# One more seven-product pair in each of row blocks three and four of a fused decoder layer, with two of their weight sums made ahead on GpSimd and VectorE

## The reference

```python
h = rms_norm(x, attn_norm_g)
proj = h @ w_in                      # 2048 x 10320 columns
q_sb, k_sb, v_sb, q_ds, k_ds, v_ds, q_ix, k_ix, w_ix, g_sb, g_ds = split(proj)
o_sb = stick_breaking_attention(q_sb, k_sb, v_sb)
o_ds = indexed_sparse_attention(rope(norm(q_ds)), rope(norm(k_ds)), v_ds, rope(q_ix), rope(k_ix), w_ix)
merged = sigmoid(g_sb) * (o_sb @ w_branch[:1024]) + sigmoid(g_ds) * (o_ds @ w_branch[1024:])
x = x + merged @ w_out
h = rms_norm(x, ffn_norm_g)
u = causal_depthwise_conv(h @ w_up, conv_w, conv_b)
x = x + (silu(gate(u)) * val(u)) @ w_down
```

## Time and profile before

| | |
|---|---|
| median of the runs | 1425.9 us |
| the profiled execution's own time | 1426.08 us |
| its span, first to last instruction | 1424.4 us |
| PE busy | 1418.9 us (100%) |
| DVE busy | 1203.8 us (85%) |
| ACT busy | 902.8 us (63%) |
| POOL busy | 329.6 us (23%) |
| DMA, mean rate | 262 GB/s |

### The profile page before, as it was taken

How to read it: one execution, slowest core, us unless ns; L and a number is a source line. 1 busy time by engine, 2 the same in 40 slices (tenths; PEclk the granted TensorE clock), 3 DMA queues, 4 the chain that set the end, 5 groups by cost and what they waited for, 6 DMA issues and landing times.

```text
span 1424.4 us, 23622 instructions
## 1 busy us (share of the span) xinstructions
PE 1418.9 (100%) x7583; PEld 1216.2 (85%) x7583; DVE 1203.8 (85%) x1591; ACT 902.8 (63%) x1302; POOL 329.6 (23%) x365
## 2 busy tenths in 40 slices
PE   9999999999999999999999999999999999999998
PEld 7888888888888888888888888888888888888887
DVE  6878998888878767887978888988889879898998
ACT  6546667566767766667665555555555556675775
POOL 2310000423232223560012222323223232100000
PEclk9999999999999999999999999999999999999999
DMA  8776665668999876569778888888888877698896
GB/s 256 243 249 183 208 197 185 194 183 293 312 337 329 285 232 209 186 239 336 258 237 279 275 292 289 279 281 279 290 289 276 280 221 233 232 318 315 312 339 250
DMA packets 151308, 373.22 MB, mean 262 GB/s; under 512 B 14048, under 2 KB 14336, under 8 KB 146768
## 3 DMA queue, kind: packets, MB, share of 16 engines
q1 hardware_dynamic: 150176, 369.93, 77.7%
q0 software_dynamic: 896, 2.42, 0.5%
q10 hardware_dynamic: 176, 0.14, 0.0%
HBM read 333.64 MB, written 38.80 MB: 261 GB/s over the span
## 4 chain that ended last, share of the span: by engine, by line
PE 99%; ACT 0%; DVE 0%; POOL 0%; issue 0%; DVEq 0%; POOLq 0%
PE bank L2320 98%; PE bank L2374 0%; PE bank L2393 0%; PE bank L2598 0%; ACT hT L837 0%; PE bank L2639 0%; DVE y L2008 0%; PE bank L2462 0%; POOL lo L2121 0%; ACT hi L820 0%; PE bank L2440 0%; DVE y L2053 0%; DVEq L243 0%; POOL ident L2101 0%; PE bank L2447 0%
## 5 line engine op out<-in xcount | busy, mean ns | idle before, releaser
L1311 DVE TENSOR_TENSOR lo<-raw,hi 128x1024 fp32r<-128x1024 f32 x338 | 436.6, 1297 | 140.4 <-ACT hi L820 138.6
L820 ACT ACTIVATE hi<-raw 128x1024 fp32r<-128x1024 f32 (+1 forms) x342 | 358.9, 1052 | 262.0 <-PE bank L2320 256.0
L2320 PE MATMUL bank<-h2T,hi 128*128 128x512 f32 x1408 | 483.3, 394 | 0.0
L2320 PE MATMUL bank<-h2T,lo 128*128 128x256 f32 x1408 | 376.8, 278 | 0.0
L2320 PEld LDWEIGHTS bank<-h2T,hi 128*128 128x128 f32 x1408 | 257.9, 188 | 53.5
L2320 PE MATMUL bank<-hT,hi 128*128 128x512 f32 (+1 forms) x784 | 272.9, 395 | 0.1
L2320 PEld LDWEIGHTS bank<-h2T,lo 128*128 128x128 f32 x1408 | 264.5, 188 | 7.8
L2320 PE MATMUL bank<-hT,lo 128*128 128x256 f32 (+1 forms) x784 | 212.6, 281 | 0.0
L1258 ACT ACTIVATE hi<-raw 128x1024 fp32r<-128x1024 f32 (+1 forms) x139 | 132.6, 974 | 64.2 <-PE bank L2320 63.2
L2320 PEld LDWEIGHTS bank<-hT,hi 128*128 128x128 f32 (+1 forms) x784 | 143.9, 187 | 29.8 <-POOL lo L2121 0.5
L1982 DVE TENSOR_TENSOR lo<-raw,hi 128x1024 fp32r<-128x1024 f32 (+1 forms) x139 | 152.2, 1124 | 16.1 <-ACT hi L1258 11.6
(11 more groups left out here) (293 smaller groups left out, 2021.8 us busy)
## 6 DMA issues: line engine op xcount, KB each, us to landing
raw<-in_w_up SPq DMA_DIRECT2D x176, 512.0 KB, 4.6
raw<-in_w_in SPq DMA_DIRECT2D x160, 512.0 KB, 4.6
raw<-in_w_down SPq DMA_DIRECT2D x61, 512.0 KB, 5.7
raw<-sums SPq DMA_DIRECT2D x54, 512.0 KB, 5.8
sums<-pre SPq DMA_DIRECT2D x19, 1024.0 KB, 6.3
raw<-in_w_branch SPq DMA_DIRECT2D x32, 512.0 KB, 4.2
pre<-in_w_down SPq DMA_DIRECT2D x19, 512.0 KB, 5.2
pre<-in_w_down SPq DMA_DIRECT2D x38, 256.0 KB, 5.6
```

The source lines that it names most:

```text
L820: act.activation(hi[s][:, 0:width], raw[s][:, 0:width], ACT.Copy)\
L1311: dve.tensor_tensor(lo[s][:, 0:width], raw[s][:, 0:width], hi[s][:, 0:width].bitcast(f32), ALU.subtract)\
L2320: return pe.matmul(o, l, r, start=start, stop=stop, skip_group_check=True)
```

## The change

Blocks 3 and 4 get five merged pairs instead of four. Two of the five, pairs 2 and 4, are of the stored kind; their weight sums (`ROW_SUMS`, one for each block and pair) are made in blocks 0 and 1 and lie in `row_sums` in DRAM. Two of these four sums are made by POOL (`pool_terms`), ahead of its work on the index keys and behind its first set of index queries, and two by DVE. The buffer for three of them is `pre_rows`; the fourth takes `pre_gates`, and the w_out sum that was made there (entry 1 of `out_sums`) moves to the branch products (`last_turn`). The activation sums of the fifth pair (`left_five`) are a third batch on DVE and ACT in block 1. The joins move from chunks 2, 8, 14, 20 of the next block to 2, 8, 17, 21.

```diff
+    ROW_SUMMED = {2: S_PAIRS, 3: S_PAIRS + 1, 4: S_PAIRS + 1}
...
     ROW_ORDER = turns(0, 4, 1, 5, 2, 6, 3, 7)
+    FIVE_ORDER = [*turns(0, 5, 1), ("stored", 2), ("plain", 6), ("summed", 3), ("stored", 4),
+                  ("plain", 7)]
+    ROW_SUMS = [(3, 2), (3, 4), (4, 2), (4, 4)]
...
-    ROW_STEPS = block_steps({b: ROW_ORDER for b in S_BLOCKS}, ROWS_AT[2], 0, False)
+    ROW_STEPS = block_steps({2: ROW_ORDER, 3: FIVE_ORDER, 4: FIVE_ORDER}, ROWS_AT[2], 0, False)
...
+    LEFT_BATCHES = [(0, 0, 2), (0, 2, 2), (0, 4, 1), (1, 0, 2), (1, 2, 2)]
...
             def rows_turn(j):
...
+                if j == 9:
+                    wait_alone(sp, ss_done, 2 * TH)
+                    wait_alone(sp, pre_stored[1], 1)
+                    row_terms(0, pre_rows, pre_landed[1])
+                if j == 14:
+                    wait_alone(sp, const_set, 6)
+                    row_store(0, pre_rows, pre_stored[1])
+                if j == 15:
+                    wait_alone(sp, pre_stored[1], 17)
+                    row_terms(1, pre_rows, pre_landed[1])
+                if j == 16:
+                    wait_alone(sp, pre_stored[0], 1)
+                    out_terms(0, pre_gates, pre_landed[0])
+                if j == 20:
+                    wait_alone(sp, const_set, 9)
+                    row_store(1, pre_rows, pre_stored[1])
+                if j == 22:
+                    wait_alone(sp, pre_stored[1], 33)
+                    row_terms(2, pre_rows, pre_landed[1])
+                if j == 24:
+                    wait_alone(sp, pre_summed, 3)
...
+                if j == 26:
+                    wait_alone(sp, pre_stored[0], 17)
+                    row_terms(3, pre_gates, pre_landed[0])
+                if j == 28:
+                    wait_alone(sp, pre_summed, 6)
+                    row_store(2, pre_rows, pre_stored[1])
+                if j == 31:
+                    wait_alone(sp, pre_summed, 9)
+                    row_store(3, pre_gates, pre_stored[0])
...
+                if j == 0:
+                    wait_alone(sp, pre_stored[0], 16 * (IN_BUFFER[0] - 1) + 1)
+                    out_terms(1, pre_gates, pre_landed[0])
...
+            JOINS_AT = (2, 8, 17, 21)
...
+            def pool_terms(e):
+
+                p, before = pre_rows, 3 + 3 * e
+                pool.wait_ge(pre_landed[1], 48 * (e + 1))
+                pool.tensor_tensor(p[:, 0:2 * GRP], p[:, 0:2 * GRP], p[:, GRP:3 * GRP], ALU.add)\
+                    .then_inc(const_set, 1)
...
+            pool_terms(0)
             pool.wait_ge(tok_done, TH)
             pool.wait_ge(cos_set, 20)
...
+                if b == 1:
+                    pool_terms(1)
```

More of the change, by code:

```diff
@@ L72, in hybrid_layer @@
     S_PAIRS = KT // 2 // 2
[L73 to L76, removed]
+    ROW_SUMMED = {2: S_PAIRS, 3: S_PAIRS + 1, 4: S_PAIRS + 1}
+    ROWS_AT = [C_ROWS, C_ROWS + 2 * CPG, C_ROWS + 4 * CPG]
+    for b in range(2, NB - 1):
+        ROWS_AT.append(ROWS_AT[-1] + 2 * CPG + 2 * ROW_SUMMED[b])
+    C_HEADS = ROWS_AT[-1] + 2 * CPG + 2 * ROW_SUMMED[NB - 1]
     ROWS_AT.append(C_HEADS)
@@ L92, in block_steps @@
             for kind, pair in order:
-                made = pair if kind == "summed" else None
-                table.append(Step(b, pair, made, chunk, raw, stored and made is not None))
+                made = pair if kind != "plain" else None
+                table.append(Step(b, pair, made, chunk, raw,
+                                  kind == "stored" or stored and made is not None))
                 chunk += 2 if made is None else 4
@@ L118, in hybrid_layer @@
             for k in range(2 if s.made is None else 4)}
-    ROW_S = [s for s in ROW_STEPS if s.made is not None]
+    ROW_S = [s for s in ROW_STEPS if s.made is not None and not s.stored]
     FAR_LAST = {b: [s for s in ROW_STEPS + OUT_STEPS if s.m == b and s.made is not None][-1].chunk
                 for b in BLOCK_END}
-    ROW_LOADS = ROW_RAWS // (SLOTS + 2)
-    ROW_SAVED = (C_HEADS - ROWS_AT[2]) // SLOTS - ROW_LOADS
+    ROW_MAIN = ROW_RAWS // (SLOTS + 2)
+    ROW_LOADS = ROW_MAIN + 1
+    assert ROW_RAWS == SLOTS * ROW_MAIN + 2 * ROW_LOADS
+    ROW_SAVED = (C_HEADS - ROWS_AT[2]) // SLOTS - ROW_MAIN
     OUT_EXTRA = OUT_RAWS // OUT_SLOTS
@@ L1000, in block_out @@
                     if c == end + 2 and b == S_BLOCKS[0]:
-                        act.wait_ge(pre_stored[0], 16 * IN_ROWS + 1)
+                        act.wait_ge(pre_stored[0], 16 * IN_ROWS[0] + 1)
+                    if c == end + 2 and b == NB - 1:
+                        act.wait_ge(pre_stored[1], 16 * IN_ROWS[1] + 1)
                     if c == end + 2 and b != NB + 1:
@@ L1482, in sums_rest @@
             def sums_rest(i):
[L1484 removed]
+                m, _, n = LEFT_BATCHES[i]
+                f, d = whole_s[m][:, 0:n], left_sraw[m][:, 0:n]
                 dve.wait_ge(left1_raw, i + 1)
@@ L1602, in joins @@
                         join(b, 1)
-                    if b < NB - 1 and 0 < at_ < 24 and at_ % 6 == 2:
-                        join(b, at_ // 6 * 2)
-                        join(b, at_ // 6 * 2 + 1)
+                    if b < NB - 1 and at_ in JOINS_AT:
+                        join(b, 2 * JOINS_AT.index(at_))
+                        join(b, 2 * JOINS_AT.index(at_) + 1)
             def weight_terms(p, landed, in_, before, k):
@@ L2555, in rows_summed @@
                 near, far = NEAR[b], FAR[b]
-                left = left_s[stage(step)]
-                s1, s2, s3, s4 = [(left[:, step.made, j, 0, :], left[:, step.made, j, 1, :])
-                                  for j in range(4)]
+                left = left_made(stage(step), step.made)
+                s1, s2, s3, s4 = [(left[:, 0, j, 0, :], left[:, 0, j, 1, :]) for j in range(4)]
                 pe.wait_ge(lo_done, c + 1)
```

140 lines of the change are left out of this document (88 added, 52 removed).

## The result

The changed kernel takes 1432.13 us (median of six runs, 1430.50 to 1433.07) against 1426.03 (six runs, 1425.77 to 1426.60): a ratio of 1.0042, 95% interval 1.0029 to 1.0054. It is slower by 6.1 us, beyond the end of the range (1430.6), where no measurable change was forecast. The profiled execution took 1432.10 us with a span of 1430.4, again 1.7 outside.

A forecast was written before the change was run, and what follows sets the result against it. The prediction took PE, idle for 5.5 of 1424.4 us, as the bound. 1426.08 - 1.36 (products) + 0.6 (blocks 3 and 4) + 2.3 (blocks 0 and 1) = 1427.6, at the median's level 1427.4 us; range 1424.3 to 1430.6.

The forecast's parts named there:

- PE's gain: Blocks 3 and 4: two plain pairs of eight products become merged pairs of seven, 2 x 0.68 = 1.36 us less.
- What POOL's adds take from DVE: Blocks 0 and 1: POOL's adds hold DVE 4.7 us a set, 9.4 for both sets between 34 and 61 us.
- The step that failed in blocks 0 and 1: Claimed chunk 15's late load, a 1.5 us stall, is contained in the scores' 2.3 us stall; the larger counts.
- the 2.3: Blocks 0 and 1: PE's stall at the scores, 9.4 us of POOL's adds less 5.5 free and 1.6 slack.
- The free time of DVE that was set against the adds: Claimed DVE has 26.3 - 20.78 = 5.5 us free in 34.5 to 60.8 us to absorb POOL's adds.
- Chunk 15's load: Blocks 0 and 1: lands at 55.2 us behind the first set's store, its result 1.5 us late for PE.
- The rival in which POOL starves: POOL's adds each wait for two DVE splits; chunk 15 lands at 58.9, PE waits 5.1 us; 1430.2 us, chance 0.20.
- at nothing by itself: Blocks 0 and 1: three more times 2 MB over the DMA engines cost nothing themselves, only as a delay.
- The step that failed in blocks 3 and 4: Claimed new waits of PE for DVE's splits of 0.3 us per block, +0.6 us, bounds none to 1.1 per block.
- DVE's 1.1 us of shortage: Blocks 3 and 4: pairs 3 and 4 with joins need 10.6 us of DVE beside 9.5 of PE.
- the moved w_out sum in the branch: Claimed hidden: it meets 6.8 free us of DVE in each 25 of the branch; uncovered it would cost 2.5 us.
- DVE's additions in 60.8 to 103.9: Claimed hidden: one set net (2.5 us) and third batch of activation sums (2.7), 5.2 us with 10.3 free.

The follow-up runs named there:

- e5: Changed kernel with POOL's second set of sums over 16 columns and the w_out term loads moved from ahead of chunk 16's load to chunk 18's; 1427.68 us.
- e8: Kernel before the change plus only POOL's three adds of 1024, 512 and 512 columns on a scratch buffer, nothing loaded, stored or used; 1427.28 us.
- e10: Changed kernel with only the three w_out term loads moved on SP from ahead of chunk 16's load to ahead of chunk 18's; 1432.11 us.
- e1: Changed kernel with POOL's second set of sums over 16 columns instead of 1024, 512 and 512; loads, stores and waits kept; 1429.39 us.
- e2: Changed kernel with DVE's adds for merged pair 3 in blocks 3 and 4 reading transposed activations, so not waiting for late weights; 1430.17 us.
- e3: Changed kernel with the third pair of join steps moved from chunk 17 to chunk 14, ahead of pair 3's first add; 1430.71 us.
- e9: Changed kernel with DVE making POOL's second set too, its four sets at chunks 19, 23, 27, 31, behind index heads' splits; joins at 14 and 21; 1426.02 us.
- e6: Changed kernel with DVE making POOL's second set at chunk 21, other sets at 25 and 28, w_out terms later, joins at 14 and 19; 1430.58 us.
- e12: Changed kernel with w_out term loads moved to chunk 18 and POOL's second set in eight adds of 256 columns, first set in four of 512; 1431.65 us.
- e11: Changed kernel with w_out term loads moved to chunk 18 and the third pair of join steps moved from chunk 17 to 14; 1430.72 us.
- e13: Changed kernel with w_out term loads moved to chunk 18 and chunk 15's load issued ahead of the store wait and second set's terms; 1431.49 us.

## Why the prediction was wrong

Set beside the prediction's sum, the profiled execution took 4.5 us more: 2.6 in blocks 3 and 4 (3.2 for 0.6), 1.5 by the clock, which is no term of the sum, and 1.0 at the stall in blocks 0 and 1 (3.3 for 2.3), less some 0.7 that it gained in its first 13 us.

- **PE's gain** was right: 7577 matmuls for 7583. Six matmuls at a third of the 0.68 us each are the 1.36; the 3.22 of new waits rests on it and is no test of it.
- **What POOL's adds take from DVE** was nearly right in size: 4.7 us a set was put, and the stretches of DVE's operations beside the second set sum to 4.0 (3.43, 1.96 and 2.31 in place of 1.22, 1.21 and 1.23); another 0.3 (0.56 twice in place of 0.42) falls to POOL's index queries behind the set. That the first set costs PE nothing, at 32.6 to 39.7 us, was not foreseen; it was put to one account with the second.
- **The step that failed in blocks 0 and 1** is "This stall lies ahead of that of the scores in the same program of PE and pushes them back too, so the larger of the two counts, not the sum: it is contained in the 2.3". On PE they are one behind the other, but on DVE they are one chain: chunk 15's `lo` first waits for its load (52.2 instead of 50.98 us for its `hi`, 1.9 later when the starts are set level) and then for POOL, and all up to `iqT_lo` comes later by both. The runs show nothing for the late load of chunk 15 alone (e5), 1.26 for the adds alone (e8) and 3.3 to 3.4 for both (after, e10): the 1.1 us of idle time and the 1.6 of slack were there once. The free time of DVE that was set against the adds, 5.5 us of 34.5 to 60.8, was also the wrong stretch; 1.1 of it lay on the chain. That 2.3 came as near to 3.3 as it did is luck: with one set for two, 1.1 us for 5.5 and the load's 1.9 left out, errors of opposite sign met. The sum of the right terms is 1.9 + 4.3 - 1.1 - 1.6 = 3.5.
- **Chunk 15's load** itself was put at 55.2 us and landed at 52.16; POOL was done with the first set at 39.75 and not 41.6. The rival in which POOL starves fell for the adds; the copies of `k_ix` behind them did starve (see the last section), where PE had time. That 1 MB more in the queue makes chunk 16's load late was costed "at nothing by itself", and is 1.25 us where nothing covers it (e1). In after it takes 8.8 us from issue to landing, 6.3 before:

```profile
raw<-in_w_in SPq DMA_DIRECT2D x1, 512.0 KB, 8.8
```

- **The clock** is no part of the sum: 1.5 us.
- **The step that failed in blocks 3 and 4** is "I take 0.3 per block", against 1.6 measured. The working went over DVE's work and PE's, and there it is nearly right: without the late load 0.44 a block are left (e2). What it missed is a wait of DVE's own. A stored pair takes four of the six raw tiles where others take two, so the loads for pair 3 go out one pair later, behind the splits of the pair two ahead, and 5 us of transfer do not fit into the three splits left. That DVE's 1.1 us of shortage had 0.9 of lead to meet it was argued from work alone, as if every operand were there. The 0.44 a block stand at one place, chunk 22, in e2, e3 and e9; their cause stays open.
- **Hidden, as predicted**: the moved w_out sum in the branch (shift 6.10 at 500, 6.10 at 630 us), DVE's additions in 60.8 to 103.9, and `k_ix`, for which PE does not wait.

## What to carry to other kernels

Find the chain of one engine that ends at a wait of the bound engine, and add everything that falls on that chain, however different its causes; count the slack at its end once, and free time only where it lies between the first delay and that end. Work on GpSimd that reads SBUF was here work on VectorE's account, at more than VectorE's own price (4.0 us for a set that VectorE makes in 2.6 in e6, 99.75 to 102.34), so place it where VectorE has nothing due soon. When a step takes more buffers of a ring, ask which load now goes out later, and who reads it first.

## What the runs showed of the hardware

POOL's adds and DVE's two-input operations take turns by the instruction, also at 1024 columns: 3.43 us for a `lo` behind an add of 2.40 that began 0.05 us earlier, 1.83 in e12 with adds of 256. This is as the Trainium skill has it ("SBUF — State Buffer", "Who interferes with whom"), for a width that no row of before showed.

The turns did not always alternate. In after POOL's two copies of `k_ix`, 96 columns each, took 5.99 us from 41.08 on, while DVE ran seven two-input operations one behind the other (40.85 to 46.47); before, the same copies took 2.45 us. What decides who is next was not tested.

```profile
41.08 5.99 POOL L2254 COPY k_ix<-tail 128x96 f32<-128x96 f32 x2 [1.33 <-DVE sin_i L1474]
```

Whether PE's clock falls behind a wait of this length differs between executions of one kernel. In e11 PE stood still at the same two places, from 63.9 to 65.9 us at the scores, and the profiled execution kept 1.00 behind it,

```profile
66.00:67.00 1.00, 1.00 (x20) 1.00 (x20) 1.00 (x2) 1.00 (x3) 0.00 (x0) 1.00 0.81 231
67.00:68.00 1.00, 1.00 (x12) 0.82 (x11) 1.00 (x1) 1.00 (x2) 0.00 (x0) 1.00 1.08 346
```

and took 1429.20 us; its other executions had a mean granted clock of 0.998 or 0.999 and took 1430.5 to 1431.4. The 1.5 us of the slow stretch after are a part of why the kernels with that wait scatter by 2 to 4 us (after 2.6, e13 3.6), and e9, without it, by 1.5. What decides it was not found.
